# Projection strips run pass by pass, with the wait for the low weights before the third pass

## The reference

```python
h = rms_norm(x, norm1_w)
(rq, rk, rv, rg, dq, dk, dv, cb, cc, cx, gates) = [h @ w_in[:, s:e] for s, e in column_bounds()]
...
merged = (g[:, :, 0] * (ret @ w_branch[0]) + g[:, :, 1] * (diff @ w_branch[1])
          + g[:, :, 2] * (conv @ w_branch[2]))
x = x + merged @ w_out
u = jnp.square(jax.nn.relu(rms_norm(x, norm2_w) @ w_up))
return x + u @ w_down
```

## Time and profile before

| | |
|---|---|
| median of 3 runs | 2386.25 us (2386.09 to 2386.81) |
| profiled execution, its own time | 2382.01 us |
| its span | 2380.2 us |
| TensorE matmul busy | 2293.7 us, 96%, 13336 matmuls |
| VectorE busy | 1068.4 us, 45% |
| ScalarE busy | 794.1 us, 33% |
| mean granted TensorE clock | 0.979 of full |

### The profile page before, as it was taken

How to read it: one execution, slowest core, us unless ns; L and a number is a source line. 1 busy time by engine, 2 the same in 40 slices (tenths; PEclk the granted TensorE clock), 3 DMA queues, 4 the chain that set the end, 5 groups by cost and what they waited for, 6 DMA issues and landing times.

```text
span 2380.2 us, 34415 instructions
## 1 busy us (share of the span) xinstructions
PE 2293.7 (96%) x13336; PEld 1917.1 (81%) x13336; DVE 1068.4 (45%) x1605; ACT 794.1 (33%) x1232; POOL 49.5 (2%) x75
## 2 busy tenths in 40 slices
PE   7999999999999998999998999999999998999996
PEld 6998994788877786888886954699999987889895
DVE  4442322434565455443444322336765446535345
ACT  3222222422454433232233244324333324323233
POOL 0000000000000000000000000002210000000000
PEclk9999999999999999999999988999999998999999
DMA  3232220222222322222222200141114221222222
GB/s 116 93 102 97 88 80 10 89 97 80 76 64 67 107 97 71 97 97 88 97 97 95 89 18 0 45 151 63 54 54 153 89 80 54 90 96 88 98 94 100
DMA packets 53757, 197.68 MB, mean 83 GB/s; under 512 B 6928, under 2 KB 7312, under 8 KB 53024
## 3 DMA queue, kind: packets, MB, share of 16 engines
q1 hardware_dynamic: 49248, 179.39, 22.8%
q10 hardware_dynamic: 3456, 13.72, 1.5%
q0 software_dynamic: 960, 3.24, 0.5%
HBM read 189.91 MB, written 6.42 MB: 82 GB/s over the span
## 4 chain that ended last, share of the span: by engine, by line
PE 93%; DVE 3%; ACT 2%; issue 1%; DMA 0%; ACTq 0%; DVEq 0%
PE ps L1416 78%; PE ps L1439 1%; PE ps L1650 1%; PE ps L1775 1%; PE ps L1560 1%; PE ps L1672 1%; PE ps L1696 1%; PE ps L1519 1%; PE ps L1588 1%; DVE xl L814 1%; PE ps L1686 1%; PE ps L1504 1%; PE ps L1656 1%; PE ps L1753 0%; PE ps L1600 0%
## 5 line engine op out<-in xcount | busy, mean ns | idle before, releaser
L1416 PE MATMUL ps<-xh,wh 128*128 128x264 f32 (+1 forms) x2976 | 788.6, 322 | 37.4 <-DVE xl L814 21.3
L1416 PE MATMUL ps<-xl,wh 128*128 128x264 f32 (+1 forms) x2976 | 779.0, 319 | 0.0
L1416 PE MATMUL ps<-xh,wl 128*128 128x264 f32 (+1 forms) x2976 | 776.9, 319 | 0.0
L342 ACT ACTIVATE wh<-wraw 128x1024 fp32r<-128x1024 f32 x338 | 356.5, 1055 | 702.0 <-PE ps L1416 700.1
L1416 PEld LDWEIGHTS ps<-xh,wh 128*128 128x128 f32 x2976 | 495.9, 190 | 93.9 <-issue 23.4
L1416 PEld LDWEIGHTS ps<-xh,wl 128*128 128x128 f32 x2976 | 493.8, 190 | 37.6
L1416 PEld LDWEIGHTS ps<-xl,wh 128*128 128x128 f32 x2976 | 494.1, 189 | 37.1 <-issue 0.5
L804 DVE TENSOR_TENSOR wl<-wraw,wh 128x1024 fp32r<-128x1024 f32 x338 | 413.6, 1224 | 205.2 <-ACT wh L342 197.5
L1416 PE MATMUL ps<-bl,wh 128*128 128x512 f32 (+1 forms) x816 | 286.3, 370 | 0.0
L1416 PE MATMUL ps<-bh,wh 128*128 128x512 f32 (+1 forms) x816 | 284.5, 368 | 1.6 <-DVE wl L804 1.6
L1416 PE MATMUL ps<-bh,wl 128*128 128x512 f32 (+1 forms) x816 | 284.7, 368 | 0.0
(11 more groups left out here) (314 smaller groups left out, 1694.4 us busy)
## 6 DMA issues: line engine op xcount, KB each, us to landing
wraw<-weights_dram SPq DMA_DIRECT2D x338, 512.0 KB, 3.2
hf<-tables_dram POOLq DMA_DIRECT2D x12, 264.0 KB, 2.9
res<-x_t_dram SPq DMA_DIRECT2D x4, 528.0 KB, 6.4
res<-x_t_dram ACTq DMA_DIRECT2D x1, 2112.0 KB, 8.6
res_dram<-res ACTq DMA_DIRECT2D x1, 2112.0 KB, 7.1
mrg_dram<-mrg ACTq DMA_DIRECT2D x1, 2112.0 KB, 8.0
mrg<-mrg_dram ACTq DMA_DIRECT2D x1, 2112.0 KB, 8.9
res<-res_dram ACTq DMA_DIRECT2D x1, 2112.0 KB, 15.3
```

The lines of the kernel that those rows point to most:

```text
L342: nc.scalar.activation(wh[:, slot], wraw[:, slot], ACT.Copy).then_inc(hi_done, 1)
L1416: last = nc.tensor.matmul(o, w[:, slot, c, :], a[:, c, tok], start=(c == chunks[0] and w is wh and a is hi), stop=(c == chunks[-1] and w i ...
```

## The change

`strip` is changed for strips that are not paced. They run all chunks of the first pass, then all of the second, then all of the third, instead of the three passes for each chunk. At their start they wait for `hi_done` instead of `lo_done`, and `lo_done` is waited for before the first matmul of the third pass. Paced strips keep their order of matmuls and wait for `lo_done` at the start.

```diff
-                pe.wait_ge(lo_done, number + 1)
+                pe.wait_ge(lo_done if ready is not None else hi_done, number + 1)
...
-                for c in chunks:
-                    if ready is not None:
+                passes = ((wh, hi), (wh, lo), (wl, hi))
+                steps = [(c, *p) for c in chunks for p in passes] if ready is not None else \
+                    [(c, *p) for p in passes for c in chunks]
+                for c, w, a in steps:
+                    if ready is None and w is wl and c == chunks[0]:
+                        pe.wait_ge(lo_done, number + 1)
+                    elif ready is not None and w is wh and a is hi:
                         pe.wait_ge(ready[0], ready[1] + c + 1)
-                    for w, a in ((wh, hi), (wh, lo), (wl, hi)):
-                        for tok, o in rows:
-                            last = nc.tensor.matmul(o, w[:, slot, c, :], a[:, c, tok],
-                                                    start=(c == chunks[0] and w is wh and a is hi),
-                                                    stop=(c == chunks[-1] and w is wl))
+                    for tok, o in rows:
+                        last = nc.tensor.matmul(o, w[:, slot, c, :], a[:, c, tok],
+                                                start=(c == chunks[0] and w is wh and a is hi),
+                                                stop=(c == chunks[-1] and w is wl))
```

## The result

| | before | changed |
|---|---|---|
| median | 2386.14 us (6 runs, 2384.59 to 2386.81) | 2366.24 us (6 runs, 2361.54 to 2368.11) |
| profiled execution | 2382.01 us, span 2380.2 us | 2367.34 us, span 2365.5 us |

The ratio is 0.9914, 95% interval 0.9901 to 0.9926: faster by 19.9 us (17.7 to 23.6). The forecast was 2375.9 us with a range down to 2370.0.

What follows compares the result with a forecast made beforehand. TensorE, busy 96% of the span, was taken as the bound. Gaps closed at strip starts (8.7 us) plus the clock (1.7 us) gave 10.4 us off the 2386.25 us median: 2375.9 us, range 2370 to 2382.5 us.

Steps and rivals of the forecast that it cites:

- (a): Starts of 320 unpaced strips: waiting for the high split only closes gaps at fourteen of them, 8.73 us gained.
- (b): Wait for the low split before the third pass of unpaced strips: already met there, 0 us.
- (c): One more wait in the middle of TensorE's stream in each of 320 unpaced strips: taken as 0 us.
- (d): Matmul order in unpaced strips: same count, shapes and loads, only neighbours change; taken as 0, bounds -7 and +7 us.
- the case in which the order costs: Matmuls stand 1 ns or so further apart when every load brings a different tile; 2383 us at its bound; chance 0.13.
- (e): TensorE's 1.2 GHz stretch at strip 270 most likely goes, 1.7 us gained, ends 0 and 3.4; strip 57 counted nothing.
- The basis: Profiled execution was 4.2 us under the median of 2386.25 us; the gain was taken off both, giving 2371.6 and 2375.9 us.
- the order helps and both slow stretches go: Matmul order helps and the 1.2 GHz stretches at strips 57 and 270 both go: 2369 us; chance 0.05.
- The slower rival: The wait before the third pass of 320 strips drains the array, 0.10 us each, 32 us: 2408 us; chance 0.06.

Runs made afterwards that it cites:

- order alone: The changed kernel, but unpaced strips wait for the low split at their start, as before: 2375.32 us against 2386.85 us, ratio 0.9953.
- one more wait: The kernel before with a wait for the long finished high split in the middle of each of 320 unpaced strips: 2386.86 us, ratio 0.9995.
- the permuted passes: The kernel before with each chunk's passes ordered wh by high, wl by high, wh by low, waits as before: ratio 0.9999.
- rows 544 apart: Activation rows 544 instead of 528 elements apart: on the kernel before, 230.2 ns at 512 columns; on the changed kernel, ratio to before 0.9950.
- chunk 0 alone: The kernel before, but every matmul of an unpaced strip takes its activations from chunk 0: 2369.99 us against 2386.94 us, one run.
- tokens outside: The changed kernel with each pass run over all chunks for the first 264 tokens, then for the second: 2378.88 us, ratio to before 0.9968.
- the four other placements: The changed kernel with activation rows 536, 544, 544 starting 16 later, and 552 elements apart: ratios to before 0.9979, 0.9950, 0.9938, 0.9929.

## Why the prediction was right or wrong

- **(a), starting on the high split.** Right, place by place in the trace. By the times, the whole change is 9 us (5 to 14) beyond order alone, for 8.7 us; that alone would be a weak test.
- **(b), the wait before the third pass.** Right: `wl` is waited for once, in a paced strip.
- **(c), 320 more waits.** Right at 0: 0.9995 with such waits alone. The Trainium skill's 50 to 100 ns for reading a semaphore (Advanced Engine Details and Errata, Miscellaneous Facts) is not paid by TensorE here: 16 us or more would have shown, and at most 1.2 us can be there.
- **(d), the order of the matmuls.** This is the step of the prediction that failed. It was taken as 0 with bounds of -7 and +7 us, its sign open, and given a rival only for the case in which the order costs. It measured 9.2 us of gain by the distances in the traces and 11.5 us (8 to 15) by the run's time, beyond the bound. In its place the runs showed that the order changes which activation addresses follow one another, and that these set the distance of 264-column matmuls (122.4 to 121.0 ns). The reason named was wrong as well: other weight tiles as neighbours did nothing (two runs), and the 3 ns between kinds at 512 columns, from which 4.5 of the 7 us came, did not turn into time: 512 columns stayed at 0.232 us. The bound on 264 columns was made from how much one order varies from stage to stage (0.02 us a strip); that says nothing about another order. It was 0.07 us.
- **(e), the clock.** Strip 270's slow stretch went, worth 1.7 us, as forecast. As a matter of one execution this holds luck: order alone lost the stretch too, with the idle time still there, and the other profiles with that idle time have it about every second time. At strip 57, 0 was taken and 0.5 us came.
- **The basis.** The profiled execution of before was 4.2 us under the median of its runs, and the forecast was carried over to the median. That was sound: two later kernels whose times equal the old one's (one more wait; the permuted passes) had profiled spans of 2385.7 and 2386.2 us.
- **The rivals.** The nearest was the one with a chance of 0.05, "the order helps and both slow stretches go", at 2369 us. The range stopped at 2370.0. The slower rival was tested and is out.

What stays open: why the order of visits to the same addresses adds or takes a further nanosecond at 264 columns (145.26 and 146.92 us against the mean of 145.62) and 2 to 3 ns at 512 columns with rows 544 apart, why chunk 0 alone has two distances, and what makes an offset cheap. Whether splitting pairs of one weight tile costs anything by itself was not tested either: the run with tokens outside changed the order of tiles and of addresses together. No run here tells.

## What to carry to other kernels

Split a combined wait so that work starts on the part that is ready first: it costs nothing where the wait is met, and only stage starts and short strips pay it back. When a change reorders a long stream of otherwise equal instructions, its cost per instruction is not known from the old order, since 1 ns on each of 6600 matmuls is 6.6 us, nearly as much as the 8.7 us of stalls; bound such a term widely in both directions. And look at where the rows of the streamed operand start: moving those of `x` was worth 13 us here on top of the change, with no instruction added. Which start is cheap has to be measured for the shape and the order at hand, since the four other placements tried gained nothing.

## What the runs showed of the hardware that was not expected

- The distance of back-to-back matmuls at 2.4 GHz depends on the start addresses of the activation stream and on what was streamed before: 227.3 to 233.4 ns for 512 columns, 120.3 to 122.7 ns for 264, as means of long stretches. The Trainium skill (TensorE: Matmul & The Clock Gate, Back-to-back issue gap) gives N / 2.4 + 2.5 ns for the gap of an isolated matmul, by estimate 215.8 ns and 112.5 ns here, and about 131 ns at N = 512 for a stream of weight loads and matmuls. Neither has a term for addresses, and no run here came that low.
- The weight tiles' order within a chunk and their place made no difference, down to 0.03 us in 350 us (two runs, both with the tiles in pairs at 264 columns).
- Executions of one kernel differ in how long TensorE runs at 1.2 GHz in the attention parts (52 and 62 us of one stage in two profiles), which moves single runs by some 5 us. Two profiles should be compared stage by stage, beside the granted clock.
